# Two attentions inside one long transformer kernel: softmax rows scaled on GpSimd, a sink column kept in PSUM, and probability buffers four deep

## The reference, cut to what matters

```
# neighbourhood attention: 8 heads of 64, each tile of 128 queries sees 256 keys
s = einsum(q, k) * 64**-0.5
s = where(mask, s + bias, -1e30)
p = softmax(s);  o = einsum(p, v)

# sliding window with sinks: 16 heads of 64 on 4 key/value heads, blocks of 128
s = einsum(q, kb) * 64**-0.5          # 128 queries x 256 keys
s = where(valid, s, -1e30)
p = softmax(concatenate([s, sink], -1))[..., :-1]   # the sink takes part in the sum only
o = einsum(p, vb)
```

## Time and profile before

| | |
|---|---|
| median of three executions | 3261.55 us |
| profiled execution | 3250.07 us, span 3248.3 us |
| TensorE busy (PE) | 3037.7 us, 94% of the span |
| GpSimd busy (POOL) | 1170.4 us, 36% |
| VectorE busy (DVE) | 1073.4 us, 33% |
| ScalarE busy (ACT) | 965.3 us, 30% |

### The profile page before, as it was taken

The page is one execution under the profiler, slowest core; times in us unless marked ns, Lnnn a source line. Parts: engine busy times, 40 slices in busy tenths (PEclk is TensorE's granted clock), DMA queues, the critical chain, the costliest instruction groups (busy, mean ns, idle before and its releaser), DMA issues.

```text
span 3248.3 us, 49144 instructions
## 1 busy us (share of the span) xinstructions
PE 3037.7 (94%) x20792; PEld 2441.5 (75%) x20792; DVE 1073.4 (33%) x1481; ACT 965.3 (30%) x1206; POOL 1170.4 (36%) x331
## 2 busy tenths in 40 slices
PE   8979999999999967999998899998999997899998
PEld 6748778887888845778887688886888865678886
DVE  4451242223211165234442421126211147541212
ACT  3153232223222246322221322223212235531222
POOL 4303343343443432322221344434444440234344
PEclk9999999999999978989998999999999999999999
DMA  4202222222222212331101122222222220122222
GB/s 183 91 6 99 91 78 100 95 91 91 91 96 99 91 52 117 134 111 46 42 26 35 55 100 91 96 98 78 91 91 104 91 81 27 41 77 97 95 92 78
DMA packets 42571, 271.82 MB, mean 84 GB/s; under 512 B 4736, under 2 KB 4864, under 8 KB 12704
## 3 DMA queue, kind: packets, MB, share of 16 engines
q1 hardware_dynamic: 39312, 252.64, 22.0%
q10 hardware_dynamic: 3088, 16.65, 1.3%
HBM read 254.58 MB, written 14.68 MB: 83 GB/s over the span
## 4 chain that ended last, share of the span: by engine, by line
issue 60%; PE 19%; POOL 15%; DVE 4%; DVEq 1%; ACT 1%; POOLq 0%; DMA 0%; ACTq 0%
POOL w_lo L469 15%; PE ps L750 8%; PE ps L578 3%; PE ps L580 2%; PE ps L579 2%; PE ps L665 1%; DVE small L1545 1%; POOL x_res L546 1%; DVEq L1544 1%; DVE work L1404 0%; PE ps L672 0%; DVE work L1487 0%; DVE ybuf L1560 0%; DVEq L1484 0%; PE ps L762 0%
## 5 line engine op out<-in xcount | busy, mean ns | idle before, releaser
L469 POOL TENSOR_TENSOR w_lo<-w_raw,w_hi 128x2048 fp32r<-128x2048 f32 x220 | 1023.8, 4654 | 1734.3 <-ACT w_hi L983 1725.3
L578 PE MATMUL ps<-act_hi,w_hi 128*128 128x512 f32 x2240 | 893.7, 399 | 44.2 <-DVE act_lo L1432 23.6
L579 PE MATMUL ps<-act_lo,w_hi 128*128 128x512 f32 x2240 | 887.7, 396 | 0.0
L580 PE MATMUL ps<-act_hi,w_lo 128*128 128x512 f32 x2240 | 887.5, 396 | 0.0
L983 ACT CAST w_hi<-w_raw 128x2048 fp32r<-128x2048 f32 x219 | 417.3, 1905 | 1039.7 <-PE ps L580 1015.6
L578 PEld LDWEIGHTS ps<-act_hi,w_hi 128*128 128x128 f32 x2240 | 424.6, 190 | 157.0 <-POOL w_lo L469 27.7
L579 PEld LDWEIGHTS ps<-act_lo,w_hi 128*128 128x128 f32 x2240 | 424.5, 190 | 99.2 <-issue 1.7
L580 PEld LDWEIGHTS ps<-act_hi,w_lo 128*128 128x128 f32 x2240 | 424.4, 189 | 99.3
L578 PE MATMUL ps<-hid_hi,w_hi 128*128 128x512 f32 x1184 | 472.1, 399 | 24.8 <-POOL w_lo L469 15.3
L580 PE MATMUL ps<-hid_hi,w_lo 128*128 128x512 f32 x1184 | 469.8, 397 | 0.0
L579 PE MATMUL ps<-hid_lo,w_hi 128*128 128x512 f32 x1184 | 469.5, 397 | 0.0
(11 more groups left out here) (251 smaller groups left out, 2389.8 us busy)
## 6 DMA issues: line engine op xcount, KB each, us to landing
w_raw<-stream SPq DMA_DIRECT2D x224, 1024.0 KB, 4.8
spill<-work ACTq DMA_DIRECT2D x5, 2048.0 KB, 6.3
scratch<-spill SPq DMA_DIRECT2D x24, 256.0 KB, 4.1
work<-bias_in SPq DMA_DIRECT2D x1, 3072.0 KB, 18.9
work<-spill SPq DMA_DIRECT2D x12, 256.0 KB, 3.1
x_res<-x_in SPq DMA_DIRECT2D x2, 1024.0 KB, 8.1
spill<-area ACTq DMA_DIRECT2D x4, 512.0 KB, 5.3
area<-spill SPq DMA_DIRECT2D x7, 256.0 KB, 2.8
```

The source lines that it names most:

```text
L469: tt(w_lo[:, s, :], w_raw[:, s, :], w_hi[:, s, :].bitcast(F32), ALU.subtract).then_inc(S["lo_made"], 1)
L578: mm(out, wh, hi[:, k, :], start=(k == 0) if begin is None else begin, stop=False)
L579: mm(out, wh, lo[:, k, :], start=False, stop=False)
L580: return mm(out, wl, hi[:, k, :], start=False, stop=end)
```

## The change

The change rewrites the attention loops of all four engines, for both attentions:

- GpSimd gets a loop `softmax(a)`: it scales the two heads' rows by the reciprocal (before on VectorE, line 1560), and in the first attention it also copies the value block into `vb_buf` (before on ScalarE, line 1128). It stands in GpSimd's program between two slabs.
- The sink is a 257th score: TensorE writes it into column 256 of the score banks with a one-column matmul, in the two of every four steps in which the pair of heads is new (t % 4 < 2; there it stays for the other two), and the mask has a 257th column of zeros. The three small VectorE and ScalarE operations on the sink (lines 1548, 1138 and 1555) are gone.
- The probabilities have four buffers, and some small operands more copies. The scores of step t wait for `at_added` (the bias added) instead of `at_max` of step t-2. The exponential waits also for the reciprocal of t-2, the negation for the exponential of t-2, the reciprocal for the scaling of four steps earlier.
- The lags change. TensorE: value turns and transposes of step t-3, product with the values for step t-4. ScalarE: both copies out of PSUM of step t-3, the output out of bank 3 of step t-5. VectorE: as before, without the scaling.
- The exponential's table is loaded by a dummy activation ahead of each attention, and one warming matmul follows the scores in the first four steps of both attentions (before in three steps of the second).

```diff
@@ -143,7 +143,9 @@
...
     ok = (s - 128 <= q) & (s > q)
-    return np.stack([np.where(ok & (s >= 128), 0, MASKED), np.where(ok, 0, MASKED)], 1).astype(np.float32)
+    table = np.zeros((P, 2, 257), np.float32)
+    table[:, :, 0:256] = np.stack([np.where(ok & (s >= 128), 0, MASKED), np.where(ok, 0, MASKED)], 1)
+    return table
@@ -199,7 +201,7 @@
...
-    "at_s", "at_max", "at_exp", "at_p", "at_pt", "at_ptsb", "at_vblk", "at_vt", "at_vtok", "at_o", "at_osb", "vtok_mm", "vtok_out",
+    "at_s", "at_added", "at_max", "at_exp", "at_recip", "at_p", "at_pt", "at_ptsb", "at_vblk", "at_vt", "at_vtok", "at_o", "at_osb", "vtok_mm", "vtok_out",
@@ -238,8 +240,15 @@
 sinks = cst[:, NCST - 16:NCST]
-p_buf = yflat[:, 1536:3072].rearrange("p (b h k) -> p b h k", b=3, h=2)
-pt_buf = yflat[:, 3072:4096].rearrange("p (b h a k) -> p b h a k", b=2, h=2, a=2)
+p_buf = yflat[:, 0:2056].rearrange("p (b h k) -> p b h k", b=4, h=2)
+pt_buf = yflat[:, 2056:3080].rearrange("p (b h a k) -> p b h a k", b=2, h=2, a=2)
+swa_mask = work[:, 18:20, :].rearrange("p k t -> p (k t)")[:, 0:514].rearrange("p (b k) -> p b k", b=2)
+NEG_MAX, SUM, MAX, RECIP = 12, 16, 20, 24
+KEYS = (256, 257)
+def tiny(at, t, count=2):
+    return small[:, at + 2 * (t % count):at + 2 * (t % count) + 2]
@@ -526,14 +535,37 @@
...
+    def softmax(a):
+        g0, steps = 16 * a, STEPS[a]
+        for t in range(steps):
+            if a == 0:
+                tile, j = divmod(t, 4)
+                if t >= 2:
+                    pool.wait_ge(S["at_vt"], t - 1)
+                v = work[:, 8 + tile, :].rearrange("p (r c) -> p r c", c=64)[:, :, NA_KEY0[j]:NA_KEY0[j] + 32]
+                nc.gpsimd.tensor_copy(vb_buf[:, t % 2, :].rearrange("p (r c) -> p r c", c=32), v).then_inc(S["at_vblk"], 1)
+            pool.wait_ge(S["at_recip"], g0 + t + 1)
+            for h in range(2):
+                p = p_buf[:, t % 4, h, 0:256]
+                inst = nc.gpsimd.tensor_scalar(p, p, tiny(RECIP, t, 4)[:, h:h + 1], None, ALU.mult)
+            inst.then_inc(S["at_p"], 1)
     lo(0, 0)
-    done = 1
+    split(1, FIRST["conv_branch"] + 1)
+    pool.wait_ge(banks_free[1], 6)
+    softmax(0)
+    done = FIRST["conv_branch"] + 1
     for name, n in POST_NO.items():
...
             done = FIRST["rwkv_o"] + 2
+        if name == "mixer1_post":
+            split(done, FIRST["o2"] + 1)
+            softmax(1)
+            done = FIRST["o2"] + 1
         split(done, end)
@@ -690,45 +722,47 @@
         g0, steps = 16 * a, STEPS[a]
-        for t in range(steps + 3):
-            if a == 1 and t == 2:
+        for t in range(steps + 4):
+            if a == 1 and t == 3:
                 pe.wait_ge(banks_free[1], FIRST["o2"] // 2)
...
                 if t >= 2:
-                    pe.wait_ge(S["at_max"], g0 + t - 1)
+                    pe.wait_ge(S["at_added"], g0 + t - 1)
                 for h in range(2):
+                    out = ps[:, SCORE_BANKS[t % 2] + h, :]
+                    if a == 1 and t % 4 < 2:
+                        mm(out[:, 256:257], c("ident"), sinks[:, 2 * (t // 4) + h:2 * (t // 4) + h + 1], start=True, stop=True)
                     for part, keys in enumerate(k_of(t, h)):
                         n = 256 // len(k_of(t, h))
-                        inst = mm(ps[:, SCORE_BANKS[t % 2] + h, n * part:n * part + n], q_of(t, h), keys, start=True, stop=True)
+                        inst = mm(out[:, n * part:n * part + n], q_of(t, h), keys, start=True, stop=True)
                 inst.then_inc(S["at_s"], 1)
-                if a == 1 and t < 3:
-                    stay_warm(1, bank=5)
-            if a == 0 and 1 <= t <= steps:
-                u = t - 1
-                if u:
-                    pe.wait_ge(S["at_vtok"], u)
-                pe.wait_ge(S["at_vblk"], u + 1)
-                for part in range(2):
-                    inst = nc.tensor.transpose(ps[:, 5, 128 * part:128 * part + 128],
-                                               vb_buf[:, u % 2, 128 * part:128 * part + 128], c("ident"))
-                inst.then_inc(S["at_vt"], 1)
-            if 2 <= t <= steps + 1:
-                u = t - 2
+                if t < 4:
+                    stay_warm(1, bank=5 if a else 4)
+            if 3 <= t <= steps + 2:
+                u = t - 3
+                if a == 0:
+                    if u:
+                        pe.wait_ge(S["at_vtok"], u)
+                    pe.wait_ge(S["at_vblk"], u + 1)
+                    for part in range(2):
+                        inst = nc.tensor.transpose(ps[:, 5, 128 * part:128 * part + 128],
+                                                   vb_buf[:, u % 2, 128 * part:128 * part + 128], c("ident"))
+                    inst.then_inc(S["at_vt"], 1)
                 pe.wait_ge(S["at_p"], g0 + u + 1)
...
                         inst = nc.tensor.transpose(ps[:, TURN_BANKS[u % 2], 256 * h + 128 * part:256 * h + 128 * part + 128],
-                                                   p_buf[:, u % 3, h, 128 * part:128 * part + 128], c("ident"))
+                                                   p_buf[:, u % 4, h, 128 * part:128 * part + 128], c("ident"))
                 inst.then_inc(S["at_pt"], 1)
-            if t >= 3:
-                u = t - 3
+            if t >= 4:
+                u = t - 4
                 pe.wait_ge(S["at_ptsb"], g0 + u + 1)
+                if a == 0:
+                    pe.wait_ge(S["at_vtok"], u + 1)
                 if u:
                     pe.wait_ge(S["at_osb"], g0 + u)
-                elif a == 0:
-                    pe.wait_ge(S["at_vtok"], u + 1)
                 for h in range(2):
@@ -873,7 +907,7 @@
...
     pe.wait_ge(S["at_osb"], STEPS[0])
-    pe.wait_ge(S["at_max"], STEPS[0])
+    pe.wait_ge(S["at_added"], STEPS[0])
     for s in range(2):
@@ -1117,43 +1151,32 @@
...
         g0, steps = 16 * a, STEPS[a]
-        for t in range(steps + 3):
-            if a == 0 and 1 <= t <= steps:
-                u = t - 1
-                tile, j = divmod(u, 4)
-                if u >= 2:
-                    act.wait_ge(S["at_vt"], u - 1)
-                v = work[:, 8 + tile, :].rearrange("p (r c) -> p r c", c=64)[:, :, NA_KEY0[j]:NA_KEY0[j] + 32]
-                nc.scalar.copy(vb_buf[:, u % 2, :].rearrange("p (r c) -> p r c", c=32), v).then_inc(S["at_vblk"], 1)
+        for t in range(steps + 5):
             if t < steps:
-                g, b, e = g0 + t, t % 3, t % 2
-                act.wait_ge(S["at_max"], g + 1)
+                act.wait_ge(S["at_max"], g0 + t + 1)
+                if t >= 2:
+                    act.wait_ge(S["at_recip"], g0 + t - 1)
                 for h in range(2):
-                    inst = af(p_buf[:, b, h, :], p_buf[:, b, h, :], ACT.Exp,
-                              bias=small[:, 12 + 2 * e + h:13 + 2 * e + h],
-                              accum_out=small[:, 16 + 2 * e + h:17 + 2 * e + h])
-                if a == 1:
-                    for h in range(2):
-                        inst = af(small[:, 24 + 2 * e + h:25 + 2 * e + h],
-                                  sinks[:, 2 * (t // 4) + h:2 * (t // 4) + h + 1], ACT.Exp,
-                                  bias=small[:, 12 + 2 * e + h:13 + 2 * e + h])
+                    p = p_buf[:, t % 4, h, 0:KEYS[a]]
+                    inst = af(p, p, ACT.Exp, bias=tiny(NEG_MAX, t)[:, h:h + 1], accum_out=tiny(SUM, t)[:, h:h + 1])
                 inst.then_inc(S["at_exp"], 1)
-            if a == 0 and 1 <= t <= steps:
-                u = t - 1
+            if a == 0 and 3 <= t <= steps + 2:
+                u = t - 3
                 act.wait_ge(S["at_vt"], u + 1)
...
                 nc.scalar.copy(vt_buf[:, u % 2, :, :], ps[:, 5, 0:256].rearrange("p (a k) -> p a k", a=2)).then_inc(S["at_vtok"], 1)
-            if 2 <= t <= steps + 1:
-                u = t - 2
+            if 3 <= t <= steps + 2:
+                u = t - 3
                 act.wait_ge(S["at_pt"], g0 + u + 1)
...
                                ps[:, TURN_BANKS[u % 2], :].rearrange("p (h a k) -> p h a k", h=2, a=2)).then_inc(S["at_ptsb"], 1)
-            if t >= 3:
-                u = t - 3
+            if t >= 5:
+                u = t - 5
                 act.wait_ge(S["at_o"], g0 + u + 1)
@@ -1327,6 +1350,7 @@
...
     hi_next(10, 0, 1)
+    preload(ACT.Exp)
     evacuated(12)
@@ -1368,9 +1392,10 @@
     root("mixer1_pre")
-    act.dma_start(work[:, 18, :].rearrange("p (b k) -> p b k", b=2), swa_in).then_inc(S["swa_loaded"], 16)
+    act.dma_start(swa_mask, swa_in).then_inc(S["swa_loaded"], 16)
     for n in range(1, 4):
         hi_next(FIRST["q2"], n // 2, n % 2)
+    preload(ACT.Exp)
     act.wait_ge(S["vtok_mm"], 1)
@@ -1533,32 +1558,27 @@
...
             if t < steps:
-                g, b = g0 + t, t % 2
-                dve.wait_ge(S["at_s"], g + 1)
-                if t >= 3:
-                    dve.wait_ge(S["at_pt"], g - 2)
```

(33 more changed lines are left out.)

## The result

The changed kernel takes 3400.82 us (median of 4 runs, 3398.19 to 3404.29); the kernel before took 3260.71 on the same chip. The ratio is 1.0431, with a 95% interval of 1.0413 to 1.0449: 140 us slower. The profiled execution took 3403.4 us, its span 3401.6 us, which is 153.3 us over the span before. The direction and the mechanism were as forecast, the size was not: the forecast was 3369 and the range ended at 3395.

What follows compares the result with a forecast made beforehand. VectorE bounds the second attention, a chain over all engines the first. Terms 21.6 + 55.1 + 5.8 + 23 + 2 = 107.5 us give 3357.6 profiled; plus 11.5, forecast 3369 us, range 3336 to 3395.

Steps and rivals of the forecast that it cites:

- The closed chain: Both attentions from step 5: emptying behind the same iteration's exponential, 5.21 and 4.94 us per step against 3.15 and 2.84.
- The fill: Start of each attention, first scores to those of step 5: 13 us in the first, 10 in the second.
- The sink's matmul: Second attention: two one-column matmuls ahead of the scores in 12 chained steps, 5.8 us; at worst double, at best 0.
- The clock: TensorE in both attentions: low level for two thirds of the 38 chains, 23 us of 35.
- The drains: End of each attention, three iterations without exponential and a last product: 8.8 us in the first, 7.9 in the second.
- The table load: First attention: the dummy moves the 1.28 us load into ScalarE's idle time, 1.3 us back once; second attention 0.
- GpSimd at nothing: Scaling on GpSimd at 0.7 us per 256 columns costs nothing under a step of 5 us.
- VectorE's relief at nothing: VectorE falls to about 1.8 us per step without scaling and sink operations, but the new lags decide the step.
- From profile to median: Whole kernel: 11.5 us added, as the median before stands that far above the profiled 3250.07.
- the 2 for slow products: Behind the first attention: 2 us for products slowed by TensorE's low clock.

Runs made afterwards that it cites:

- e3: Changed kernel with three extra 256-column matmuls, results unread, behind the transposes of each chained step: 3353.67 us, one run, ratio 1.030.
- e1: Changed kernel with ScalarE emptying bank 3 of step t-4 in place of t-5: 3247.89 us, ratio 0.9976.
- e2: Kernel before, with ScalarE emptying bank 3 one iteration later in the second attention only: 3360.16 us, one run, against 3254.65.
- g3: Changed kernel, lag of 5 kept, with the emptying of bank 3 moved ahead of ScalarE's exponential: 3249.66 us, one run, against 3253.35.
- e4: Changed kernel with both one-column sink matmuls ahead of both heads' scores: 3374.69 us, one run, against 3254.65 for the kernel before.
- f4: Changed kernel, all lags kept, with VectorE scaling the rows in place of GpSimd: 3409.05 us, one run, ratio 1.046.
- f3: Changed kernel with emptying of t-4, both sinks ahead of the scores and scaling on VectorE: 3241.88 us, ratio 0.9952; with scaling on GpSimd 3239.11 us.

## Why the prediction was wrong in its number

Step by step, against the profile:

- **The closed chain.** Right. Between the scores of step 5 and 6 of the first attention, still at full clock, it is 5.24 us (185.70 to 190.94); the forecast said 5.21. e3 gives 5.00 for 4.94. e1, e2 and g3 show the cause from three sides.

```profile
185.70 0.70 PE L737 MATMUL ps<-work 64*128 64x256 f32 x4
...
190.94 0.70 PE L737 MATMUL ps<-work 64*128 64x256 f32 x4
```

- **The fill.** 13.2 us in the first for 13; 17.1 us in the second for 10 (2733.25 to 2750.37): 7 us missed. I counted the warming matmuls at full clock; the granted clock was 0.70 on average there, a warming matmul took 2.07 us in place of 1.12, and three of the five steps (0, 1 and 4) carry sinks.

```profile
2740.14 2.07 PE L674 MATMUL ps<-cst 128*128 128x512 f32 x2
```

- **The sink's matmul. This is the term of the sum that missed most.** "Two stand ahead of the scores in half of the steps [...] 12 x 0.48 = 5.8 us. At worst they double at half clock". Measured: 12 x 2.15 = 25.8 us, and 1.25 for step 5, still at full clock, which my count of 12 left out: 27 us. I priced the added instruction by its own row and not what it does to its neighbours. The two do not both stand ahead of the scores, as the forecast has it: by the diff the second stands between the two heads' scores, and there it takes away their overlap, which costs as much again as the two matmuls (e4). With 27 in its place the forecast would have been 3390 us.
- **The clock. This is the second step that failed.** I put two thirds of the chains at the low level. In the second attention every window from 2760 on is at 0.50: 25 chains x 1.03 and 0.5 for the chain that began at full clock, 26 us where the forecast had 16; in the first 7.5 us for 6. The drains, which I left at full clock, took 17.3 and 18.8 us behind the last scores where the forecast, one chain included, had 12.9 and 14.0: 9 us in all. The row nearest to 41% busy, with 7.13 of 20 us, had said 0.50, and for two thirds I had no row. The Trainium skill, "TensorE: Matmul & The Clock Gate", section "HAM oscillation — how this bites in real kernels", tells of a matmul kernel in which each burst after a wait for a DMA starts throttled. The traces agree and go further: with waits of 2.6 us in front of the product the low level held through the bursts too, 0.50 in the steady chain here and 0.57 in e2. The windows of the changed kernel, one of the first attention and two of the second, the last of them in the drain:

```profile
204.00:212.00 8.00, 4.80 (x23) 3.05 (x22) 2.90 (x8) 2.42 (x9) 2.87 (x5) 0.50 0.00 0
2850.00:2900.00 50.00, 31.80 (x156) 24.49 (x156) 11.19 (x29) 12.09 (x42) 12.76 (x14) 0.50 0.00 1
2937.00:2949.00 12.00, 8.74 (x52) 5.85 (x52) 0.00 (x0) 2.53 (x7) 2.24 (x3) 0.50 0.00 1
```

- **The table load.** Right: the first exponential starts at 175.57 where it started at 177.01, and no load stands in front of it.
- **GpSimd at nothing.** Right (f4), although its price of 0.92 us per head was above the 0.7 taken. **VectorE's relief at nothing.** Right.
- **From profile to median.** I added 11.5 us, as the profiled execution before stood that far below its median. The profiled execution after stands 2.6 us above its own. By profiles the forecast was 46 us short; by medians the 140 us measured stand against 107.5.

The misses add up: 7 for the fill, 21 for the sinks, 10 for the second's clock and 1.5 for the first's, and 8 in the drains (9, less the 1 that the two thirds already held for their two chains). That is some 48, less the 2 for slow products, which the rest of the kernel doesn't show: 46 us for the 46. By cause it is otherwise: a step with sinks costs 1.25 us more at full clock and 2.15 at half, so about 11 us of the sinks' 21 are the low clock again. The clock then makes some 30 of the 48 and the lost overlap, with the thirteenth step, 10; the fill's 7 hold both.

## What to carry to other kernels

In a pipeline written by hand, list for each engine what stands ahead of each operation in the same iteration, and follow every wait for a single buffer through that list: one emptying behind one exponential made a chain over two steps into a chain over one, and with what followed from it cost 4.3%, all of which came back with it (e1, g3). The closed chain cost twice here, since it left TensorE idle and took its clock (e3). Take the level of the nearest row, not a mean. An added instruction is priced with its neighbours, with the overlap that it ends, and the order on an engine (the emptying ahead of the exponential, g3) can be worth more than moving work to an idle engine (f3).

## What was new about the hardware

One-column matmuls over all 128 rows cost 0.94 us a pair at half clock ahead of the scores of two heads of 64 rows each (e4), and 2.15 with the second between the heads; with one row in place of 128, in the half of the rows that the head uses, the pair of sink matmuls fell from 0.54 to 0.31 us at full clock. GpSimd scales 256 fp32 columns by a per-row factor in 0.92 us, where two inputs over 512 columns took 1.27 us: one input was not cheaper per column. Extra matmuls that nobody reads, put where TensorE sat idle in the closed chain, raised its clock and made the kernel some 41 us faster (e3, one run).
